# First block: the memory's sum of squares two jobs later, and the modulation rounds spread over the attention steps in halves

## What is computed

```python
sh1, sc1, g1, sh2, sc2, g2 = split(silu(c) @ w_mod + b_mod, 6)     # the same for the context
hx = rmsnorm(x, norm1_g) * (1 + sc1) + sh1
hc = rmsnorm(ctx, norm1_g) * (1 + csc1) + csh1
qa, ka, va, qb, kb, vb = split_proj(hx @ w_in)                     # and k, v of the context
ya = differential attention (4 heads);  yb = windowed attention (8 heads, with a sink)
x = x + g1 * (concat(ya, yb) @ w_out)
hx2 = rmsnorm(x, norm2_g) * (1 + sc2) + sh2
x = x + g2 * moe(hx2)          # 32 experts, 4 of them for each token
# second block: its memory attention starts with rmsnorm(mem, norm_mem) @ w_mem_kv
```

## Time and profile before

| | us |
|---|---|
| time, median of 3 runs | 1635.29 |
| lowest and highest | 1635.18, 1637.16 |
| time of the profiled execution | 1635.24 |
| its span in the profile | 1633.3 |
| PE busy | 1562.3 (96%) |
| DVE, ACT, POOL busy | 557.5, 437.7, 29.9 |
| DMA, mean over the span | 322 GB/s |

### The profile page before, as it was taken

How to read it: one execution, slowest core, us unless ns; L and a number is a source line. 1 busy time by engine, 2 the same in 40 slices (tenths; PEclk the granted TensorE clock), 3 DMA queues, 4 the chain that set the end, 5 groups by cost and what they waited for, 6 DMA issues and landing times.

```text
span 1633.3 us, 22528 instructions
## 1 busy us (share of the span) xinstructions
PE 1562.3 (96%) x9460; PEld 937.8 (57%) x9460; DVE 557.5 (34%) x1083; ACT 437.7 (27%) x885; POOL 29.9 (2%) x41
## 2 busy tenths in 40 slices
PE   6989899999999999999999999999899999999998
PEld 5876683343333333333434434344399988899986
DVE  3947531112011111111201101111255564468774
ACT  3435530111011101101101101110345563356553
POOL 0210000000000000000000000000010100000000
PEclk9999999999999999999999999999999999999999
DMA  9517668999999999999999999999955534434530
GB/s 390 207 52 310 248 276 337 409 433 432 431 433 431 432 434 429 433 430 431 432 431 429 432 431 428 435 426 432 421 162 179 176 124 155 163 147 164 198 129 26
DMA packets 28519, 526.60 MB, mean 322 GB/s; under 512 B 3235, under 2 KB 4387, under 8 KB 6772
## 3 DMA queue, kind: packets, MB, share of 16 engines
q1 hardware_dynamic: 26816, 520.52, 76.5%
q0 software_dynamic: 1024, 3.15, 0.9%
q10 hardware_dynamic: 596, 1.71, 0.3%
HBM read 524.28 MB, written 1.08 MB: 322 GB/s over the span
## 4 chain that ended last, share of the span: by engine, by line
PE 72%; DMA 19%; DVE 5%; ACT 2%; issue 1%; SPq 1%; POOL 0%; DVEq 0%; ACTq 0%; POOLq 0%
PE ps L689 70%; DMA ring<-in_w_down 18%; DMA ring<-in_first 1%; PE ps L834 1%; SPq L600 0%; PE ps L1027 0%; DVE ring_r L1851 0%; PE ps L1020 0%; PE ps L1249 0%; DVE mx L1968 0%; DVE arena L1929 0%; ACT arena L1679 0%; DMA small<-in_small 0%; DVE arena L1919 0%; ACT w_high L1413 0%
## 5 line engine op out<-in xcount | busy, mean ns | idle before, releaser
L689 PE MATMUL ps<-ring,arena 128*64 128x512 f32 (+1 forms) x3840 | 707.5, 533 | 23.1 <-DMA ring<-in_w_down 14.7
L689 PEld LDWEIGHTS ps<-ring,arena 128*64 128x64 f32 (+1 forms) x3840 | 236.6, 132 | 439.2 <-issue 404.9
L689 PE MATMUL ps<-arena 128*128 128x128 f32 (+8 forms) x1732 | 302.7, 408 | 13.2 <-DVE arena L2235 4.7
L689 PEld LDWEIGHTS ps<-arena 128*128 128x128 f32 (+3 forms) x1732 | 175.1, 176 | 141.1 <-issue 121.3
L689 PE MATMUL ps<-arena_r,w_high 128*128 128x256 f32 x1360 | 247.8, 285 | 0.0
L2129 DVE TENSOR_SCALAR arena<-ps 128x512 f32<-128x512 f32 x32 | 22.1, 692 | 570.9 <-PE ps L689 570.9
L689 PEld LDWEIGHTS ps<-arena_r,w_high 128*128 128x128 f32 x1360 | 212.2, 192 | 2.9 <-issue 1.7
L689 PE MATMUL ps<-arena_r,ring_r 128*128 128x256 f32 x680 | 192.3, 283 | 0.0
L2205 DVE TENSOR_TENSOR ring_r<-ring,w_high 128x1024 fp32r<-128x1024 f32 x120 | 142.3, 1221 | 94.8 <-ACT w_high L1648 94.3
L1585 ACT ACTIVATE arena<-ps 128x256 f32<-128x256 f32 x32 | 12.3, 384 | 450.1 <-PE ps L1020 450.1
L1648 ACT ACTIVATE w_high<-ring 128x1024 fp32r<-128x1024 f32 x120 | 121.3, 1053 | 34.8 <-PE ps L689 32.6
(11 more groups left out here) (222 smaller groups left out, 1100.3 us busy)
## 6 DMA issues: line engine op xcount, KB each, us to landing
ring<-in_w_gate_up SPq DMA_DIRECT2D x62, 4096.0 KB, 19.8
ring<-in_w_down SPq DMA_DIRECT2D x29, 4096.0 KB, 18.6
ring<-in_second SPq DMA_DIRECT2D x32, 2048.0 KB, 8.0
ring<-in_first SPq DMA_DIRECT2D x17, 2048.0 KB, 17.9
ring<-in_w_down SPq DMA_DIRECT2D x12, 1024.0 KB, 12.4
ring<-in_w_gate_up SPq DMA_DIRECT2D x8, 1024.0 KB, 8.2
arena<-in_memory SPq DMA_DIRECT2D x4, 1024.0 KB, 6.1
ring<-in_first SPq DMA_DIRECT2D x4, 512.0 KB, 11.2
```

What stands on the lines that cost most here:

```text
L689: return nc.tensor.matmul(out_, lhsT, rhs, start=start, stop=stop, **kw)
```

## The change

Four things are edited. `MEM_SUM = 10` takes the place of `MEM_JOB + 4`: PE's matmul on the memory's sum, ACT's root and DVE's scaling move from behind job 8 to behind job 10. On ACT, the split of part 2 comes ahead of the context's first two squares, and the other squares move back by two. On DVE, the splits behind job 3 come right after `rope(1)`, ahead of `rope(2)` and `rope(3)`. The modulation rounds 4 to 11 move from steps 4, 5, 7, 8, 10, 11, 13, 15 to steps 5, 7, 9, 11, 13, 15, 16, 17; rounds 4 to 9 are done in two halves of 16 matmuls, the first half in the step before; rounds 10 and 11 stay whole. No computation is added or dropped.

```diff
@@ tables
+        MEM_SUM = 10
-        ADA_STEPS = (4, 5, 7, 8, 10, 11, 13, 15)
+        ADA_STEPS = (5, 7, 9, 11, 13, 15, 16, 17)
+        ADA_HALVES = 6
@@ tensor
-            def ada_rows(n, bank):
+            def ada_rows(n, bank, k0=0, k1=KC):
...
-                pe.wait_ge(slot_full[SLOT_1[u]], filled(u))
-                if n:
-                    pe.wait_ge(ada_row, n)
-                for k in range(KC):
+                if k0 == 0:
+                    pe.wait_ge(slot_full[SLOT_1[u]], filled(u))
+                    if n:
+                        pe.wait_ge(ada_row, n)
+                for k in range(k0, k1):
...
-                last.then_inc(ada_mm, 1)
+                if k1 == KC:
+                    last.then_inc(ada_mm, 1)
...
-                if n == MEM_JOB + 4:
+                if n == MEM_SUM:
                     pe.wait_ge(root_set, NORM_CTX + 1)
                     pe.wait_ge(sq_used, KC * (NORM_MEM + 1))
...
+                if a == ADA_STEP:
+                    pe.wait_ge(proj_dve, len(ROPED))
+                    pe.wait_ge(proj_act, len(COPIED))
+                if ada_at(a + 1) is not None and ada_at(a + 1) - 4 < ADA_HALVES:
+                    ada_rows(ada_at(a + 1), 1, 0, KC // 2)
                 if ada_at(a) is not None:
-                    if a == ADA_STEP:
-                        pe.wait_ge(proj_dve, len(ROPED))
-                        pe.wait_ge(proj_act, len(COPIED))
-                    ada_rows(ada_at(a), 1)
+                    ada_rows(ada_at(a), 1, KC // 2 if ada_at(a) - 4 < ADA_HALVES else 0, KC)
@@ scalar
+            split_hi1(2)
             act.wait_ge(ctx_in, 16)
             ctx_square(0)
             ctx_square(1)
-            for p in range(2, HI_PARTS):
-                split_hi1(p)
-                ctx_square(p)
+            split_hi1(3)
+            ctx_square(2)
+            ctx_square(3)
@@ vector
-            for n in range(1, 4):
-                rope(n)
+            rope(1)
             splits(3)
+            rope(2)
+            rope(3)
...
-                if n == MEM_JOB + 4:
+                if n == MEM_SUM:
                     inverse_rms(NORM_MEM)
...
+            for n in (10, 11):
+                ada_columns(n, 0)
             dve.wait_ge(ada_col, 12)
```

## The result

The changed kernel takes 1627.64 us (median of 6 runs, 1625.93 to 1628.93), the one before 1635.24 (6 runs); the ratio is 0.9948, with a 95% interval from 0.9938 to 0.9958. So it is faster by 7.6 to 9.8 us, half a per cent. The profiled execution took 1625.93 us with a span of 1623.9, against 1635.24 and 1633.3: 9.3 us less.

The account below looks back on a forecast made before the run. PE's chain was taken as the bound (72%, DMA 19%), with the stages before the experts forming one line. Gains of 7.1 + 0.65 + 0 + 2.9 = 10.65 us off 1635.24 gave 1624.6 us, range 1621.0 to 1628.5.

Parts of the forecast that it names:

- Part 1: Memory's sum moved behind job 10 in the projections: PE's wait for POOL and the low clock go, 7.1 us.
- statement on cover: Behind job 10, DVE is free 1.3 us before its first maxima; were that gone, each us of lateness costs one.
- Part 2: Splits ahead of rope(2): jobs 6 and 7 run 1.29 us earlier, 0.65 us remain at job 8, between 0 and 1.3.
- Part 3: ACT's split ahead of the context's squares: job 1's wait mostly goes, job 4 waits longer; 0 us, between -0.5 and 0.3.
- Part 4: Modulation rounds in halves in the attention: PE's idle time gets filled, gain 2.9 us, between -1.0 and 6.0.
- Queues: SP's load of w_out's second half: issued at about 175.5, lands near 193.4, wanted at about 202, 8 us of cover.
- The rival that ends slower: w_out's second half reaches the output projection late: slower from 34 us issue-to-landing on, 1641 at 40; chance 0.03.
- Signs: PE's trace: no wait over 0.7 us in jobs 8 to 11, first scores about 107.5; attention steps above 4.5 wrong.
- the attention's waits only move: In the attention, ACT's copies and DVE's chain stay last, the tail eats the rest: gain 7.75, 1627.5; chance 0.17.
- The one on the clock: Clock falls, or stops falling, elsewhere: none at the router, 1623.0, or one in the tail, +2.6, 1627.2; chance 0.15.
- Its other half: At the router the clock's fall, worth 1.6 us, may not come: 1623.0.

Follow-up runs that it names:

- warm_wait: The kernel before with 9 matmuls on constants ahead of PE's wait for the memory's sum, the wait itself kept; 1634.03 us, ratio 0.9989.
- sum_behind_11: The changed kernel with the memory's sum one job later still, behind job 11; 1627.35 us, ratio 0.9944.
- splits_only: The kernel before with only the splits behind job 3 moved ahead of rope(2); 1635.48 us, ratio 0.9998.
- rounds_by_15: The changed kernel with rounds 4 to 7 in halves up to step 11 and rounds 8 to 11 whole in steps 12 to 15; 1627.40 us, ratio 0.9950.
- rounds_only: The kernel before with only the new places and halves of the modulation rounds; 1634.55 us, ratio 0.9994.

## Why the prediction was right, point by point

The forecast was 1624.6 us with a range of 1621.0 to 1628.5, 10.65 us faster. The median lies inside, 3.0 us above the forecast; the profiled execution lies 1.3 above it. By the marks, 9.4 us were won instead of 10.65: the sum lost 0.1 us in part 2, 0.6 in part 3 and 0.65 in part 4. The large term, part 1, was right, and that carried the forecast.

**Part 1** was right in mechanism and size: 7.1 us forecast, 7.14 measured alone. Its split between wait and clock holds too, 4.5 and 2.6 against 4.8 and the 2.33 of `warm_wait`; the clock's part differs between executions by 1 us, which the single trace could not say. Its statement on cover was wrong. "Were it gone, each us of lateness would cost one" took the first maxima for a paced chain, but jobs 12 and 13 stand between the first scores and the next thing that PE wants of DVE, and `sum_behind_11` pays nothing for 3.65 us. The cover ahead of the maxima was 2.00 us, not 1.3.

**Part 2** was right: 0.56 us against 0.65, and job 8 waits 0.77 us (0.6 forecast). `splits_only` shows what the text left open, that the gain exists only behind part 1.

**Part 3** is the first step that failed. "An earlier PE only waits longer there: 0" is what happened on PE (job 4's wait is 1.21), but I followed PE and not ACT's own order. Two squares in a row need the two-place buffer free twice, and the split behind them waits with them. The term is a loss of 0.67 us on the mean (0.3 to 1.0), where the text took 0 with a loss of 0.5 as its lower bound. Job 1's wait did shrink, from 0.94 to 0.33 us, and the longer wait at job 4 took it back, as said. Between the two profiled executions 0.57 us of it shows at job 4, because after happened to start 0.23 us earlier.

**Part 4** was right in mechanism and 0.65 us too high: 2.24 to 2.26 instead of 2.9. The mis-sized term is the half round. I took half of 1.88 us, and it is 1.01 (131.42 to 132.43), so six rounds in halves cost 0.8 us more. The text had the small gaps shrink instead, which makes up its step from 2.4 to 2.7 us of waits to a gain of 2.9. The waits did a little better than forecast, from 6.02 us to 2.96 (3.3 to 3.6 forecast), and 3.06 less 0.8 is the gain measured. One by one they came as listed: 0.33 at step 4, 0.35 at step 7 (0.6 forecast), 0.69, 0.58 and 0.78 at the end, and the tail 9.13 us (9.3 forecast). That the round of step 17 takes the tail's wait away is shown by `rounds_by_15`, 1.1 us; but it lies behind the table load, beside the copies that follow it, and not beside the load.

**Queues.** The second half of `w_out` was forecast to be issued at about 175.5 and to land near 193; it was 177.75 and 192.55, and wanted at about 203. The rival that ends slower stayed far away.

**Signs.** Of those listed, job 6's missing wait, the clock of 1.00 up to the router and the sum that waits for nobody came. Job 4 waits 1.21 us (about 1), the first scores come at 108.22 (107.5) and the output projection at 189.12 (188). Two were overstepped a little: job 8's 0.77 us against "no wait over 0.7", and step 9, which lasts 4.59 us against the 4.5 that was to be a sign of being wrong. It is the first step with both halves of the turned probabilities, and it has a wait of 0.23 us for ACT.

**Rivals.** That the attention's waits only move is refuted by `rounds_only`. The one on the clock came true for part of the executions, at 3.1 us where the text had allowed 2.6, and at the router and not in the tail: the spread of 1625.3 to 1628.9 us is about as wide as that one term. That it makes most of the distance between median and forecast (1.7 of 3.0 us lie between the profiled execution and the median) is inferred, since both profiles of the changed kernel show the shortest case. Its other half, 1623.0 without the fall, was over-priced: the fall is worth 0.4 us there and not 1.6, by one pair of profiles. The Trainium skill (TensorE: Matmul & The Clock Gate, "What's actually happening") calls the moment at which the throttle is released run-variable. The traces agree for the half clock behind the sum's wait, which cost 1.35 to 2.33 us.

## What to carry to other kernels

Price a long wait on TensorE (4.59 us here) twice, by its length and by the matmuls behind it that run at half clock; matmuls on constants in the wait measure the second price alone, and moving the waiting instruction behind work that does not depend on it recovers both. Work that is spread into steps which other engines pace is nearly free, but count what each cut costs (0.07 us a half here), and put what is left where PE waits for the slower engine at the end. A low clock ahead of a wait for another engine costs less than the time it takes from PE; look at what PE reaches next before pricing it. Where an instruction moves on an engine with a two-place buffer in its path, follow that engine's own order to whatever is queued behind the new stall, and compare sub-microsecond edits by marks in the trace and not by medians when executions differ by 3 us.

## What the runs showed of the hardware that I had not expected

The clock falls at the router in all 14 profiles, and with the router unchanged the time at half clock was 3.4, 6.8 or 10.2 us for the same work; the cases end 49.4, 51.0 and 52.5 us behind the start of the output projection. In 11 of the 12 profiles with an unchanged router the first fall comes at the end of a row of 32 matmuls with 32 columns (3.65 us in after) or up to 0.9 us behind it, although PE's last wait lies 33 us or more back. In the twelfth, `rounds_only`, the clock stayed at 1.00 over the same row. With the row broken up it fell behind a wait of 1.98 us instead, while job 6's wait of 1.29 us in the kernel before brings no fall. The half clock behind the sum's wait likewise ended at about 97 us in one execution and at 99 in another, with the wait the same to 0.15 us (4.74 and 4.59).
